# A new order of the last third of the hybrid stage, on all engines

## The reference, cut to what matters

```python
def hybrid_mixer(h, pos, w_in, w_out, sink, lb, norm_w):
    aq, ak, av, bq, bff, bfb, bi, bg = jnp.split(h @ w_in, offs, axis=-1)
    o_a = window_attention(...)      # 8 heads of 64, band of 128, ALiBi, a sink in the softmax
    o_b = hgrn2_bidir(...)           # 4 heads of 128, a decaying scan forward and backward
    return jnp.concatenate([o_a, o_b], axis=-1) @ w_out

# in hgrn2_bidir, behind the two scans
    o = rms_norm(o, norm_w[:, None, :])
    return o * jax.nn.silu(hg)
```

## Time and profile before

| | us |
|---|---|
| median of three timed runs | 1075.19 (1074.13 to 1075.66) |
| span of the profiled execution | 1072.5 |
| TensorE busy in it | 1028.6 (96%) |
| VectorE busy | 797.6 (74%) |
| ScalarE busy | 495.1 (46%) |
| GpSimd busy | 73.0 (7%) |

### The profile page before, as it was taken

One profiled execution on the slowest core, in us unless ns is written; L12 is line 12 of the kernel. 1 busy time (PEld: TensorE's weight loads), 2 busy tenths in 40 slices (PEclk: granted clock), 3 DMA queues, 4 the chain that ended last, 5 costly groups with the idle time before them and its releaser, 6 DMA issues.

```text
span 1072.5 us, 13324 instructions
## 1 busy us (share of the span) xinstructions
PE 1028.6 (96%) x5104; PEld 857.2 (80%) x5104; DVE 797.6 (74%) x1147; ACT 495.1 (46%) x721; POOL 73.0 (7%) x161
## 2 busy tenths in 40 slices
PE   8899999999998999999999999999988899999996
PEld 7788888789976778888887888888878777888885
DVE  5678889777797687888778778877756677666455
ACT  2443434446767453434435344443456554434340
POOL 1000000001311000000000000000441000000000
PEclk9799999999999999999999999999899999999999
DMA  9899999736332489979848988972223338666531
GB/s 370 338 338 357 365 379 385 254 120 210 111 119 89 157 327 350 325 271 344 292 152 339 322 306 279 382 267 82 85 79 118 119 136 305 230 229 219 196 118 39
DMA packets 72321, 254.80 MB, mean 238 GB/s; under 512 B 8769, under 2 KB 10049, under 8 KB 72258
## 3 DMA queue, kind: packets, MB, share of 16 engines
q1 hardware_dynamic: 68946, 242.91, 62.8%
q0 software_dynamic: 3168, 10.52, 3.1%
q10 hardware_dynamic: 144, 0.52, 0.2%
HBM read 252.85 MB, written 1.07 MB: 237 GB/s over the span
## 4 chain that ended last, share of the span: by engine, by line
PE 79%; DVE 9%; issue 3%; ACT 3%; DMA 3%; POOL 1%; SPq 0%; DVEq 0%; ACTq 0%; POOLq 0%
PE bank L1600 24%; PE bank L1604 24%; PE bank L1603 24%; DVE w_lo L1039 3%; DMA w_raw<-in_w_dram 2%; PE bank L1966 2%; ACT w_hi L768 1%; PE bank L1914 1%; PE bank L1703 1%; PE bank L1726 1%; DMA w_raw<-in_ada_w_dram 1%; POOL arena L722 1%; PE bank L1693 1%; ACT arena L783 1%; PE bank L1595 1%
## 5 line engine op out<-in xcount | busy, mean ns | idle before, releaser
L1039 DVE TENSOR_TENSOR w_lo<-w_raw,w_hi 128x2048 fp32r<-128x2048 f32 (+2 forms) x162 | 355.5, 2216 | 28.3 <-ACT w_hi L768 28.3
L1600 PE MATMUL bank<-w_hi,hT_hi 128*128 128x512 f32 (+3 forms) x880 | 353.1, 401 | 4.3 <-DVE hT_lo L1078 4.3
L1604 PE MATMUL bank<-w_lo,hT_hi 128*128 128x512 f32 (+3 forms) x880 | 343.5, 390 | 0.0
L1603 PE MATMUL bank<-w_hi,hT_lo 128*128 128x512 f32 (+3 forms) x880 | 342.8, 390 | 0.0
L768 ACT ACTIVATE w_hi<-w_raw 128x2048 fp32r<-128x2048 f32 (+2 forms) x162 | 300.2, 1856 | 37.0 <-DMA w_raw<-in_w_dram 29.7
L1600 PEld LDWEIGHTS bank<-w_hi,hT_hi 128*128 128x128 f32 x880 | 168.7, 192 | 35.1 <-DVE hT_lo L1078 3.6
L1604 PEld LDWEIGHTS bank<-w_lo,hT_hi 128*128 128x128 f32 x880 | 168.2, 191 | 34.4
L1603 PEld LDWEIGHTS bank<-w_hi,hT_lo 128*128 128x128 f32 x880 | 168.8, 192 | 30.4
L838 ACT ACTIVATE arena<-bank 128x256 f32<-128x256 f32 x88 | 33.7, 383 | 313.2 <-PE bank L1604 313.2
L1050 DVE SCALAR_TENSOR_TENSOR arena<-arena,c_row 128x1024 f32<-128x1024 f32 x136 | 161.9, 1220 | 9.0 <-DMA cols<-in_cols_dram 8.1
L1600 PE MATMUL bank<-w_hi,fT_hi 128*128 128x512 f32 x352 | 138.3, 393 | 3.6 <-DVE fT_lo L1533 3.6
(11 more groups left out here) (231 smaller groups left out, 876.1 us busy)
## 6 DMA issues: line engine op xcount, KB each, us to landing
w_raw<-in_w_dram SPq DMA_DIRECT2D x310, 512.0 KB, 5.3
arena<-in_ada_w_dram SPq DMA_DIRECT2D x140, 512.0 KB, 7.1
gate_row<-gate_scratch POOLq DMA_DIRECT2D x6, 512.0 KB, 4.8
arena<-in_ln_g_dram POOLq DMA_DIRECT2D x6, 512.0 KB, 5.0
arena<-in_ln_b_dram POOLq DMA_DIRECT2D x6, 512.0 KB, 7.6
w_raw<-in_w_dram SPq DMA_DIRECT2D x8, 256.0 KB, 2.9
w_raw<-in_w_dram SPq DMA_DIRECT2D x8, 192.0 KB, 2.8
gate_row<-in_ada_w_dram SPq DMA_DIRECT2D x2, 512.0 KB, 12.9
```

The costliest lines, as they stand in the source:

```text
L1039: nc.vector.tensor_tensor(w_lo[:, j0 % RING, 0:n], w_raw[:, j0 % RAW, 0:n], w_hi[:, j0 % RING, 0:n].bitcast(F32), ALU.subtract)\
L1600: mm = nc.tensor.matmul(dst, a_hi, b_hi, start=start, stop=False)
L1603: nc.tensor.matmul(dst, a_lo, b_hi, start=False, stop=False)
L1604: return nc.tensor.matmul(dst, a_hi, b_lo, start=False, stop=stop)
```

## The change

In `hybrid_plan` the list behind `hi 15` is written out by hand in another order. `attention_step` gets a fourth stage `E n`, directly behind `S n`, and ScalarE takes the exponentials there; in the part that is written by hand `E n` has places of its own. `out (2, 0)` is issued in two halves, with `V 7` between them. Everything up to `S 5` stays in its order on every engine, as does everything behind `owin 1`, save that `out (2, 0)` now stands ahead of it. `mla_plan` yields the `E` steps too, and no engine does anything in them.

```diff
@@ -358,17 +358,12 @@
             yield from (("Z", 6), ("Z", 7), ("proj", 13), ("hg", 0), ("hg", 1), ("A", 6), ("O", 5), ("M", 6))
             yield from attention_step(4, 8)
             yield from (("lo", 14), ("A", 7), ("O", 6), ("M", 7), ("hi", 15))
-            yield from attention_step(5, 8)
-            yield from (("O", 7), ("sq", 0), ("sq", 1), ("owin", 0))
-            yield from attention_step(6, 8)
-            yield from (("lo", 15), ("gate", 0), ("out", (0, 0)), ("hi", 16))
-            yield from attention_step(7, 8)
-            yield from (("hnorm", 0), ("hnorm", 1), ("out", (1, 0)), ("lo", 16), ("hi", 17))
-            yield from attention_step(8, 8)
-            yield from (("hT", 0), ("hT", 1))
-            yield from attention_step(9, 8)
-            yield from (("owin", 1), ("out", (2, 0)), ("lo", 17), ("out", (3, 0)), ("hi", 18), ("lo", 18), ("out", (0, 1)),
-                        ("out", (1, 1)), ("out", (2, 1)), ("next", 0), ("out", (3, 1)))
+            yield from (("S", 5), ("P", 4), ("V", 3), ("E", 5), ("O", 7), ("S", 6), ("owin", 0), ("V", 4), ("P", 5), ("S", 7),
+                        ("sq", 0), ("E", 6), ("sq", 1), ("gate", 0), ("out", (0, 0)), ("E", 7), ("P", 6), ("V", 5), ("hi", 16),
+                        ("out", (1, 0)), ("hnorm", 0), ("hnorm", 1), ("lo", 15), ("hT", 0), ("hT", 1), ("P", 7), ("V", 6),
+                        ("out", (2, 0, 0)), ("lo", 16), ("V", 7), ("out", (2, 0, 1)), ("hi", 17), ("owin", 1), ("lo", 17),
+                        ("out", (3, 0)), ("hi", 18), ("lo", 18), ("out", (0, 1)), ("out", (1, 1)), ("out", (2, 1)), ("next", 0),
+                        ("out", (3, 1)))
 
         OWIN = (0, 3)
 
@@ -445,7 +440,7 @@
 
         def attention_step(n, units):
 
-            for stage, m in (("S", n), ("P", n - 1), ("V", n - 2)):
+            for stage, m in (("S", n), ("E", n), ("P", n - 1), ("V", n - 2)):
                 if 0 <= m < units:
                     yield stage, m
 
@@ -992,7 +987,7 @@
                             nc.scalar.activation(e_neg[b], e_mid[b], ACT.Exp, scale=-1.0)
                             nc.scalar.activation(e_dec[b], f_cum[d][:, h, :], ACT.Exp)
                             nc.scalar.activation(e_mid[b], e_mid[b], ACT.Exp).then_inc(hexp_ready, 1)
-                        elif stage == "S":
+                        elif stage == "E":
                             attention_exp(m)
                         elif stage == "P":
                             act.wait_ge(p_tr, m + 1)
@@ -1889,10 +1884,10 @@
                                                      ident[:, :])
                         mm.then_inc(o_tr, 1)
                     elif stage == "out":
-                        i, t = m
+                        i, t, *q = m
                         if m == (0, 0):
                             pe.wait_ge(proj_read, 14)
-                        out_project(s, i, t, HOUT, range(4), {0: OWIN[t] + 1, 2: t + 2})
+                        out_project(s, i, t, HOUT, range(4), {0: OWIN[t] + 1, 2: t + 2}, q or (0, 1))
 
             def enter_first(t):
 
```

## The result

The changed kernel took 1066.52 us (median of four runs, 1065.25 to 1066.75), the kernel before 1074.66 beside it: a ratio of 0.993, 95% interval 0.9912 to 0.9949 (the two medians alone divide to 0.9924). Later runs narrowed it: eleven of the changed kernel have a median of 1066.36 us, 69 of the kernel before one of 1074.25 (1071.14 to 1077.49), a gain of 7.9 us.

A forecast was written before the change was run, and what follows sets the result against it. TensorE, 96% busy, could gain only where it stood still; afterwards a VectorE chain was to bound the stretch. Span 1072.5 less 5.8 gives 1066.7, plus 2.7 around the span 1069.4 us; range 1067.7 to 1072.3.

The forecast's parts named there:

- the walk: Hybrid stage's tail: new order added up with old durations and hand-overs; next stage's transposes at 361.5 instead of 367.3 us.
- No wait at P5, P6 or P7: Sign at three transposing steps: the forecast is wrong if TensorE waits over 0.5 us there for the exponentials.
- the way through slot 17's high half: ScalarE's and VectorE's chain to tile 0's normalisation: sets the new end at 361.5 us, TensorE waiting 1.3 us.
- The gain of the stretch: From the last scan output product to the next stage's transposes: 367.3 - 361.5 = 5.8 us won.
- the clock does not set the end: Old order's tail: half clock from 333 to 338 us costs nothing, as VectorE's chain runs beside it.
- rival 2: Clock falls once in the new mixed stretch, moving the end by 0.4 to 1.7 us: 1069.8 to 1071.1 us; chance 0.22.
- the 2.7 us "around the span": Whole kernel: time outside the profiled span, timed median 1075.19 against span 1072.5 us, added to the forecast.
- rival 1: At the stretch's end TensorE stays the bound: transposes at 360.2, gain 7.1, time 1068.1 us; chance 0.13.
- nothing was given back behind the stretch: Answers the rival that a later stage waits for something unmoved, taking 3.7 of 5.8 us; chance 0.06.
- the load of slot 18: Rival: it lands late and delays tile 0's normalisation, gain gone at 13.1 us, 1078 us at 16; chance 0.02.

The follow-up runs named there:

- tail_early: Changed kernel with slot 17's high half directly behind V6 on ScalarE and its low half ahead of the attention-output transposes' low part; 1063.77 us, ratio 0.9902.
- again: The changed kernel once more, without an edit; median 1066.32 us, ratio 0.9926.
- fill_before: Kernel before, order kept, with 16 idle matmuls filling TensorE's gaps between the last scan output product and the last attention-output transposes; 1073.41 us, ratio 0.9994.
- exp_in_s: Changed kernel with the exponentials of S5, S6 and S7 back directly behind the maxima on ScalarE; 1068.00 us, ratio 0.9946.
- best: Changed kernel reordered so that TensorE never waits from O7 to the next stage's transposes; 1064.50 us, then 1063.10 us in a second set.
- head_alone: Kernel before with the new order only up to V5 and slot 16's high half, the tail nearly the old one; 1070.60 us, ratio 0.9974.
- owin_first: Changed kernel with product (2,0) put back whole behind the last attention-output transposes; 1068.59 us, ratio 0.9951.
- before_again: The kernel before once more, without an edit; median 1074.02 us, ratio 0.9999.

## Why the prediction was right in the stretch and wrong in the time

**Right: the walk.** Counted from O7, measured against said: product (0,0) after 3.95 us (3.8), the normalisation on VectorE after 9.11 (8.9), the last attention-output transposes after 17.90 (17.7), the next stage's transposes after 30.62 (30.3). No wait at P5, P6 or P7. VectorE's and ScalarE's rows, beside the earlier trace rows: the second power 1.43 us instead of 1.02, the high half of slot 17 where it was expected, VectorE's wait for the copy behind it 2.93 us, and ScalarE takes slot 18 without waiting for data.

```profile
339.10 2.16 DVE L1380 SCALAR_TENSOR_TENSOR arena<-bank,rms,arena 128x128 f32<-128x128 f32 x8
...
349.93 0.69 DVE L1487 TENSOR_TENSOR hT_lo<-bank,hT_hi 128x512 fp32r<-128x512 f32 x1 [2.93 <-ACT hT_hi L1017]
```

```profile
347.50 1.91 ACT L763 ACTIVATE w_hi<-w_raw 128x2048 fp32r<-128x2048 f32 x1
349.30 0.59 ACT L1017 ACTIVATE hT_hi<-bank 128x512 fp32r<-128x512 f32 x1
349.77 1.92 ACT L763 ACTIVATE w_hi<-w_raw 128x2048 fp32r<-128x2048 f32 x1
```

The forecast's bound, the way through slot 17's high half, was the right one: `tail_early` moved slot 17's two halves alone and won 1.4 us in the stretch. The gain of the stretch was put at 5.8 us and is 5.5 against the first trace. The 0.3 us grow along the way (0.15 us at product (0,0), 0.2 at the normalisation); no single step stands out.

**Wrong: "the clock does not set the end".** This was read from one execution in which the fall was hidden. In the other form of the old order, two of four traces, falls cost 2.4 us on TensorE's path, which the prediction had put at nothing. The prediction looked for the risk of falls in the new order (rival 2, 0.22), and they were in the old one; the change takes them away with the gaps. In the mean of the four traces that is 37.3 - 36.1 = 1.2 us more gain. The traces show the mechanism and its price; how often the costly form comes is known from four traces only.

**Wrong: the starting point.** The median of three runs, 1075.19, lay 0.9 us above that of 69 runs. The term that carried this into the sum is the 2.7 us "around the span". In the later runs, where each time is listed beside its span, the difference is 1.95 us in the mean (`again`'s traced execution: 1064.29 and 1062.4). 1072.5 and 1.95 give 1074.4, close to the median of the 69: the profiled execution was an ordinary one, and the three runs were a little slow.

**Open: 1.2 us.** The medians differ by 7.9 us, the mean stretches by 37.3 - 30.6 = 6.7. From these two kernels alone the rest could be nothing: the interval of `again`, 0.9911 to 0.9941, stands for gains from 6.3 to 9.6 us, and 6.7 lies inside. The share of the costly form matters too: the stretch alone gives 5.5 us if that form never comes and 7.9 if it always comes, while `fill_before` speaks against more than 1.9 us for the falls. But the variants say that a part is real. The median time less the 1.95 us around the span and less the stretch is an estimate of what lies outside: 1035.0 us for the kernel before, 1035.4 for `fill_before`, 1033.8 for the changed kernel, and 1032.9, 1032.6 and 1033.0 for `exp_in_s`, `tail_early` and `best` (both sets), the other new orders in whose stretch no trace has a fall. So the new orders have about 1 to 2 us less outside. The traces overstate this for the changed kernel: its three traced executions (1065.25, 1064.29 and 1064.90 us) are all faster than its median. The cause stays open. For these two kernels falls of the clock outside the stretch hardly explain it: the mean granted clock, listed for 65 runs of the kernel before and eleven of the changed one, is 0.9837 and 0.9863; I estimate from it 34.9 and 29.2 us at half speed, 5.7 less, and the stretch's own falls are 5.1 of that in the mean of the four traces (3.4 or 6.8 us each).

Together: 1069.4 - 0.9 (start) - 1.2 (clock) - 1.2 (open) + 0.3 (stretch) = 1066.4. The open part is what is left over, so that the sum meets the median shows nothing.

**The range** failed for the same reasons: its lower end let only the new order differ (rival 1, 1068.1), and held the old order's time for fixed. With one of the two errors mended the forecast becomes 1068.5 or 1068.2, inside the range; with both it becomes 1067.3, below 1067.7. The rule of the Trainium skill (TensorE: Matmul & The Clock Gate, "A second HAM failure mode: psum-queue depth-cycling"), that frequent short idles make the clock swing, is borne out in part, and for the old order: waits of 1.3 to 2.6 us, none of them long, were followed by falls in all four of its traces and in `head_alone` and `owin_first`, while the new order's 0.9 and 1.2 us were followed by none in three traces. But a wait of 1.80 or 1.33 us was followed by a fall in some traces and by none in others, so no length of a wait decides it alone. None of the rivals came: VectorE's way did bound the end, the clock was never low in the new stretch, nothing was given back behind the stretch (702.7 to 705.0 us there, against 703.4 to 705.8), and the load of slot 18 was in time.

## What to carry to other kernels

Where engines run fixed orders, walking the new order with start-to-start times from the old trace gave the length of the stretch to 0.3 us here as long as the clock did not fall, and the same walk finds the next order (`best`) as well. But measure the stretch of the old kernel in more than one trace before you price its removal: gaps of 1.3 to 2.6 us on TensorE may cost their own length in one execution and 2.4 us more in the next (1.5 to 1.6 us for one fall that stands wholly on TensorE's path), and a hidden fall of the clock in your one profile is no proof that falls are free. Closing a gap on TensorE's path can be worth its length and the falls behind it.

## What the runs showed of the hardware

The same program has different falls of the clock in different executions, and one fall changes what follows: half speed behind the first gap makes TensorE late, which shortens the second gap from 2.56 to 1.33 us. In the two traces with the first fall none came at the second gap; in the two without it one did. Sixteen matmuls that compute nothing kept the clock at 1.00 through the old order in the one trace of `fill_before`, without making the stretch longer. And a wait of 1.33 us at the same instruction was followed by a fall in `before_again` (1.10 us for the four transposes) and by none in the first trace (0.66 us): such a wait has no fixed price.
